# Mixture-of-experts blocks of 32 tokens in four column groups instead of 64 tokens in two

## The reference

```python
def grouped_moe(h, router_w, router_bias, w1, w3, w2):
    s = jax.nn.sigmoid((h @ router_w).astype(jnp.float32))
    ...                                   # best group of 4 experts, best 2 in it, weights wts
    combine = jnp.sum(jax.nn.one_hot(idx, N_EXPERTS) * wts[..., None], axis=1)
    for e in range(N_EXPERTS):
        he = (jax.nn.silu(h @ w1[e]) * (h @ w3[e])) @ w2[e]
        out = out + combine[:, e:e + 1] * he
```

```
layer 0: 83 69 44 52 91 105 52 24 81 70 62 63 55 57 65 51
layer 1: 11 31 42 52 25  35 40 26 12 14  7 27 73 40 60 17
```

## Time and profile before

| | |
|---|---|
| median of the runs | 1326.32 us |
| the profiled execution: its own time / span | 1325.98 us / 1324.2 us |
| PE busy / granted clock, mean | 1071.6 us (81%) / 0.882 of full speed |
| PEld, DVE, ACT, POOL busy | 490.0, 470.8, 230.0, 159.9 us |
| mean DMA rate | 240 GB/s |
| experts, layer 0: first product to barrier passed | 487.60 to 777.12 us |
| experts, layer 1: first product to barrier passed | 1062.32 to 1304.70 us |

### The profile page before, as it was taken

The page is one execution under the profiler, slowest core; times in us unless marked ns, Lnnn a source line. Parts: engine busy times, 40 slices in busy tenths (PEclk is TensorE's granted clock), DMA queues, the critical chain, the costliest instruction groups (busy, mean ns, idle before and its releaser), DMA issues. The chain is left out here.

```text
span 1324.2 us, 13657 instructions
## 1 busy us (share of the span) xinstructions
PE 1071.6 (81%) x4448; PEld 490.0 (37%) x4449; DVE 470.8 (36%) x902; ACT 230.0 (17%) x451; POOL 159.9 (12%) x272
## 2 busy tenths in 40 slices
PE   3899999777677649999998918998768489788891
PEld 1344444355444423333333306453553433223230
DVE  1167405666231432222222245624733412112223
ACT  2101121354210101111111102112520111111110
POOL 2111000000100001221221121000010012111111
PEclk8999999786688759999999968998869599888896
DMA  9978777800200534898989659113004479999973
GB/s 345 370 244 283 279 274 275 334 1 1 80 16 16 223 126 163 342 422 365 425 359 423 254 197 380 65 64 143 1 4 164 166 272 420 400 417 422 418 321 121
DMA packets 69134, 317.64 MB, mean 240 GB/s; under 512 B 7596, under 2 KB 7832, under 8 KB 55516
## 3 DMA queue, kind: packets, MB, share of 16 engines
q1 hardware_dynamic: 55760, 284.70, 54.6%
q0 software_dynamic: 9568, 20.54, 4.4%
q10 hardware_dynamic: 3756, 11.73, 2.3%
HBM read 311.10 MB, written 14.75 MB: 246 GB/s over the span
## 5 line engine op out<-in xcount | busy, mean ns | idle before, releaser
L1481 PE MATMUL ps<-ring,area 128*64 128x512 f32 x1296 | 301.0, 615 | 20.7 <-DMA ring<-in_w 16.8
L1481 PE MATMUL ps<-ring,HT 128*128 128x512 f32 (+1 forms) x672 | 295.1, 596 | 4.8 <-issue 3.0
L1481 PE MATMUL ps<-area 128*64 128x512 f32 (+5 forms) x904 | 251.6, 532 | 18.1 <-DVE area L1408 12.3
L1481 PEld LDWEIGHTS ps<-ring,HT 128*128 128x128 f32 x672 | 128.7, 195 | 158.0 <-issue 154.8
L1481 PEld LDWEIGHTS ps<-ring,area 128*64 128x64 f32 x1296 | 91.9, 141 | 189.6 <-issue 171.5
L1426 DVE COPY area<-ps 128x512 f32<-128x512 f32 x42 | 29.0, 691 | 330.1 <-PE ps L1698 330.1
L1481 PEld LDWEIGHTS ps<-area 128*64 128x64 f32 (+2 forms) x904 | 114.3, 200 | 53.3 <-issue 30.0
L1481 PE MATMUL ps<-HT,area 128*64 128x512 f32 x208 | 97.4, 623 | 10.0 <-DMA area<-in_w 10.0
L956 ACT ACTIVATE area<-ps 64x512 f32<-64x512 f32 x40 | 23.7, 592 | 432.1 <-PE ps L1481 432.1
L1060 DVE SCALAR_TENSOR_TENSOR area<-area,CW 128x512 f32<-128x512 f32 (+1 forms) x120 | 68.8, 614 | 3.9
L956 ACT ACT_TABLE_LOAD x40 | 51.3, 1283 | 41.9 <-DVEq L1419 41.2
(11 more groups left out here) (180 smaller groups left out, 814.3 us busy)
## 6 DMA issues: line engine op xcount, KB each, us to landing
ring<-in_w SPq DMA_DIRECT2D x66, 2048.0 KB, 10.2
ring<-in_w_ada SPq DMA_DIRECT2D x24, 2048.0 KB, 14.4
ring<-in_w_in SPq DMA_DIRECT2D x10, 2048.0 KB, 20.1
HT<-in_w SPq DMA_DIRECT2D x10, 2048.0 KB, 10.4
area<-in_w SPq DMA_DIRECT2D x10, 2048.0 KB, 10.5
area<-in_w SPq DMA_DIRECT2D x20, 1024.0 KB, 8.4
ring<-in_w_out SPq DMA_DIRECT2D x4, 2048.0 KB, 14.8
area<-expert_rows ACTq DMA_DIRECT2D x12, 512.0 KB, 6.7
```

The lines of the kernel that those rows point to most:

```text
L1481: return t_.matmul(out, lhsT, rhs, start=first, stop=last_)
```

## The change

`SLOT` becomes 32, so NG = 4 column groups and NW = 256: groups 0 and 1 take the two halves of w1, groups 2 and 3 those of w3; in the second product each group takes 256 of the 1024 outputs. A gather moves 128 quarter rows. NCH, the number of 128-column pieces in NW, falls from 4 to 2 and with it the transposes per block. `CB` becomes 52 (`BMAX` 48 and 4), `PEEL` 4. w2 is laid out so that a partition reads two pieces of 8 KB instead of one of 16 KB.

The gathered rows and ym get two buffers each, used in turn, with one semaphore per buffer. DVE now copies the gathered rows from xg to `xs` (`copy_x`), and PE transposes xs. gather(n) waits for the copy of block n-2. POOL works in pairs of blocks, and the number of pairs is (blocks + 3) >> 1, so that POOL gathers and scatters a few blocks past the last one; their rows are all out of bounds.

```diff
-SLOT = 64
+SLOT = 32
-CB = BMAX + 1
-PEEL = 3
+CB = BMAX + 4
+PEEL = 4
...
-        w2_v = A["w2"].rearrange("l e (p k) n -> l e p k n", p=P)
+        w2_v = A["w2"].rearrange("l e (a p k) n -> l e p a k n", p=P, a=2)
...
-                def gather(n):
+                def gather(n, r):
 
-                    if not isinstance(n, int) or n:
-                        hold(pool, xt_full[l], n, pool_passed)
-                    g.tensor_copy(gidx, TG[:, bass.ds(n, 1)]).then_inc(gidx_set[l], 1)
+                    if not isinstance(n, int) or n >= 2:
+                        hold(pool, xs_rdy[l], n - 1, pool_passed)
+                    g.tensor_copy(gidx[r], TG[:, bass.ds(n, 1)]).then_inc(gidx_set[l], 1)
...
-                blocks = pool.value_load(nb[0:1, E_N:E_N + 1], min_val=E_N, max_val=BMAX)
+                pairs = pool.value_load(nb[0:1, E_N + 1:E_N + 2], min_val=PEEL, max_val=BMAX // 2 + 2)
...
-                with pool.Fori(PEEL, blocks + 1) as n:
-                    gather(n)
-                    scatter(pool.snap(sent))
-                    pool.reg_add(sent, sent, 1)
-                for t in range(2):
-                    scatter(pool.snap(sent) + t)
-                hold(pool, scat[l], 16 * blocks, pool_passed)
+                with pool.Fori(PEEL // 2, pairs) as i:
+                    for r in range(2):
+                        gather(2 * i + r, r)
+                        scatter(pool.snap(sent) + r, r)
+                    pool.reg_add(sent, sent, 2)
+                for t in range(PEEL):
+                    hold(pool, scat[l][t % 2], pool.snap(sent) * 8 + 16 * (t // 2), pool_passed)
+                    scatter(pool.snap(sent) + t, t % 2)
+                for r in range(2):
+                    hold(pool, scat[l][r], 16 * pairs, pool_passed)
...
+                dve.drain()
+                v.tensor_scalar(nbi[:, 0:1], nb[:, E_N:E_N + 1], 3.0, None, ALU.add)
+                dve.drain()
+                v.tensor_scalar(nb[:, E_N + 1:E_N + 2], nbi[:, 0:1], 1, None, ALU.arith_shift_right)
...
+                def copy_x(n):
+
+                    if isinstance(n, int):
+                        dve.wait_ge(gath[l][n % 2], 16 * (n // 2) + 16)
+                        at_ = n % 2 * NW
+                    else:
+                        hold(dve, gath[l][0], 16 * ((n + 2) // 2), dve_passed)
+                        hold(dve, gath[l][1], 16 * ((n + 1) // 2), dve_passed)
+                        at_ = n % 2 * NW
+                    v.tensor_copy(xs, xg[:, bass.ds(at_, NW)]).then_inc(xs_rdy[l], 1)
...
-                    v.tensor_copy(ym, ps[:, B_W2, :]).then_inc(y_rdy[l], 1)
+                    if isinstance(m, int):
+                        if m >= 2:
+                            dve.wait_ge(scat[l][m % 2], 16 * (m // 2))
+                    else:
+                        hold(dve, scat[l][0], 16 * (m // 2), dve_passed)
+                        hold(dve, scat[l][1], 16 * ((m - 1) // 2), dve_passed)
+                    v.tensor_copy(ym[:, bass.ds(m % 2 * NW, NW)], ps[:, B_W2, 0:NW]).then_inc(y_rdy[l], 1)
...
                     v.tensor_copy(gT.rearrange("p c s -> p (c s)"), ps[:, B_GT, 0:NCH * 64]).then_inc(gt_rdy[l], 1)
-
+                    copy_x(b + 2)
+
+                copy_x(0)
                 copy_xT(0)
+                copy_x(1)
...
                 copy_y(dve.snap(copied))
+                dve.drain().then_inc(y_rdy[l], 3)
...
-                    hold(pe, gath[l], 16 * n + 16, pe_passed)
+                    hold(pe, xs_rdy[l], n + 1, pe_passed)
                     for a in range(NCH):
-                        last = t_.transpose(ps[:, B_XT, a * P:(a + 1) * P], xg[:, a * P:(a + 1) * P], ident)
+                        last = t_.transpose(ps[:, B_XT, a * P:(a + 1) * P], xs[:, a * P:(a + 1) * P], ident)
```

More of the change, by code:

```diff
@@ L349, in hybrid_moe_kernel @@
         nbi = cut(E_N).bitcast(i32)
-        nb = cut(E_N + 1).bitcast(i32)
+        nb = cut(E_N + 2).bitcast(i32)
         TG = cut(CB).bitcast(i32)
@@ L353, in hybrid_moe_kernel @@
         TW = cut(CB)
-        gidx = cut(1).bitcast(i32)
-        sidx = cut(1).bitcast(i32)
-        xg = cut(NW)
+        gidx = [cut(1).bitcast(i32) for _ in range(2)]
+        sidx = [cut(1).bitcast(i32) for _ in range(2)]
+        xg = cut(2 * NW)
+        xs = cut(NW)
         YM_AT = at[0]
@@ L362, in hybrid_moe_kernel @@
         gT = cut(NCH * 64).rearrange("p (c s) -> p c s", c=NCH)
-        ym = cut(NW)
+        ym = cut(2 * NW)
         EX_AT = max(at[0], 2816)
@@ L437, in hybrid_moe_kernel @@
         nb_ready = sem("counts_ready")
-        gath = sems("tokens_gathered", DEPTH)
+        gath = [sems(f"tokens_gathered_{l}", 2) for l in range(DEPTH)]
+        xs_rdy = sems("tokens_copied", DEPTH)
         xt_full = sems("xT_product", DEPTH)
@@ L447, in hybrid_moe_kernel @@
         y_rdy = sems("y_copied", DEPTH)
-        scat = sems("y_scattered", DEPTH)
+        scat = [sems(f"y_scattered_{l}", 2) for l in range(DEPTH)]
         dve_passed = sem("dve_waits_passed")
@@ L724, in gather @@
                     hold(pool, gidx_set[l], n + 1, pool_passed)
-                    pool.indirect_dma_start(xg, None, h2_rows, bass.IndirectOffsetOnAxis(ap=gidx, axis=0),
-                                            bounds_check=routed(l) * NG - 1, oob_is_err=False).then_inc(gath[l], 16)
-                def scatter(m):
+                    pool.indirect_dma_start(xg[:, r * NW:(r + 1) * NW], None, h2_rows, bass.IndirectOffsetOnAxis(ap=gidx[r], axis=0),
+                                            bounds_check=routed(l) * NG - 1, oob_is_err=False).then_inc(gath[l][r], 16)
@@ L730, in scatter @@
+                def scatter(m, r):
                     hold(pool, y_rdy[l], m + 2, pool_passed)
-                    g.tensor_copy(sidx, TS[:, bass.ds(m, 1)]).then_inc(sidx_set[l], 1)
+                    g.tensor_copy(sidx[r], TS[:, bass.ds(m, 1)]).then_inc(sidx_set[l], 1)
                     hold(pool, sidx_set[l], m + 1, pool_passed)
-                    pool.indirect_dma_start(y_rows, bass.IndirectOffsetOnAxis(ap=sidx, axis=0), ym, None,
-                                            bounds_check=2 * routed(l) * NG - 1, oob_is_err=False).then_inc(scat[l], 16)
+                    pool.indirect_dma_start(y_rows, bass.IndirectOffsetOnAxis(ap=sidx[r], axis=0), ym[:, r * NW:(r + 1) * NW], None,
+                                            bounds_check=2 * routed(l) * NG - 1, oob_is_err=False).then_inc(scat[l][r], 16)
@@ L736, in _ @@
                 for n in range(PEEL):
-                    gather(n)
-                blocks = pool.value_load(nb[0:1, E_N:E_N + 1], min_val=E_N, max_val=BMAX)
+                    gather(n, n % 2)
+                pairs = pool.value_load(nb[0:1, E_N + 1:E_N + 2], min_val=PEEL, max_val=BMAX // 2 + 2)
                 sent = pool.alloc_register(f"pool_blocks_{l}")
                 pool.reg_mov(sent, 0)
-                with pool.Fori(PEEL, blocks + 1) as n:
-                    gather(n)
-                    scatter(pool.snap(sent))
-                    pool.reg_add(sent, sent, 1)
```

8 lines of the change are left out of this document (3 added, 5 removed).

## The result

The changed kernel takes 1315.49 us (median; 1310.0 to 1317.96) beside 1325.16 for the kernel before in the same runs: ratio 0.9917, 95% interval 0.9897 to 0.9937. It is faster by 9.7 us; 26 were forecast. The profiled execution lies at 1315.83, its span is 1314.0 against 1324.2.

A forecast was written before the change was run, and what follows sets the result against it. TensorE was taken to bound layer 0 and the weights layer 1; from 1325.98, -27.5 (layer 0), -12.5 (layer 1), +3.3 (starts) and +10.5 (stage ends) sum to -26, so 1300 us, range 1284 to 1332.

The forecast's parts named there:

- The block, 6.1: Both expert stages: a 32-token block takes 24 steps of 0.215 plus 0.94, 6.1 us; first product 3.6, second 1.9.
- Rival (b): Expert products: weight loads don't hide, step 0.272, block 7.5, total 1351 us; chance 0.13 together with other slower ways.
- rival (a): Expert products: TensorE's sequencer binds, priced at a step of 0.25 and block of 6.9, total 1323 us; chance 0.09.
- Rival (c): Expert stages: POOL or the gather and scatter transfers bind, block 6.9, total 1323 us; chance 0.08.
- half the transposes fall away ... leaving 0.94: Each block: the 1.28 us lost between steps to transposes and the changes around them shrinks to 0.94.
- The weights have become the bound, the last product ends near 740: Layer 0: weight loads bind instead of TensorE; last product near 740 instead of 767.7, -27.5 us.
- behind it stand two blocks and the last second product: Layer 0's end: 14.8 us of work remain after w3 of expert 15 lands at 725.5.
- Rival (d): Weight loads in both layers: 2% slower from 8 KB w2 pieces and more indirect DMAs, +8, 1308 us; chance 0.10.
- The forecast's 5.4: Layer 0 weight stream: 5.4 us per load over 36 issues, from w2 of expert 3 to w2 of expert 15.
- Layer 1, -12.5: Layer 1's expert stage: weights bind before and after; earlier stream start and shorter work behind the last w3 give -12.5 us.
- Empty scatters, +10.5: Ends of both stages: trailing empty scatters delay the last issue by 6.3 and 4.2 us, +10.5.
- Starts, +3.3: Stage starts: copy xs, tiny DVE operations and larger tables cost 1.9 in layer 0 and 1.4 in layer 1.

The follow-up runs named there:

- e1: Changed kernel with two tiny transposes in place of the two TensorE drains at an expert's first block; 1311.81 us, ratio 0.9913.
- e8: Changed kernel, drains kept, each expert weight load cut to a small part, only layer 0 read; 254.63 us from first product to last y copy.
- e9: Changed kernel with expert weight loads cut to a small part and without the drains, only layer 0 read; 246.46 us from first product to last y copy.
- e10: Changed kernel with full weight loads but only two of eight row groups of the first product made; layer 0 247.93 us from first product to last y copy.
- e11: Kernel before with blocks of 32 tokens and the new w2 layout, without second buffers or copy xs; 1379.18 us.
- e12: Changed kernel with blocks of 64 tokens again, keeping second buffers, copy xs and the loop of block pairs; 1342.88 us, ratio 1.014.
- e4: Kernel before, blocks of 64 tokens, with the changed kernel's drains put in at experts' first blocks; 1333.85 us, ratio 1.0079.

## Why the prediction was wrong

- **The block, 6.1: right.** 6.09 inside an expert, products 3.66 and 1.93, a step 0.215. Rival (b) (weight loads don't hide, 0.272 a step) and rival (a) (0.25) are out. The step's eight instructions went out one each 0.027, twice as densely as any row before had shown. Of the two ways that the Trainium skill names (TensorE: Matmul & The Clock Gate, What happens when you issue a matmul), the 62 ns of a matmul decoded in microcode would have made a step 0.248. The trace, with 0.215, agrees with the hardware decoder alone.
- **Rival (c): out.** Mid-stage waits of TensorE for gathered rows are absent, a gather lands in 6.5 (median) and 8.2 at most in e1; y copies waited 4.3 in layer 0 for scatters, off the path.
- **The block between experts: wrong, and hidden.** The step "half the transposes fall away ... leaving 0.94" overlooked the drains that take their place at each expert's first block, 0.69 a pair by e8 and e9. As long as the weights bind they cost nothing clear of noise in layer 0 (e1).
- **"The weights have become the bound, the last product ends near 740": right mechanism, two terms mis-sized. This is the step that failed.** From e1, which has the blocks as forecast: the rate, 5.49 instead of 5.4 per load, +3.4; and "behind it stand two blocks and the last second product", 14.8 behind the landing of expert 15's w3, +6.3. The load on which the end really hangs is expert 14's w3, with five blocks behind it. The forecast's own numbers would have shown 2.4 of the 6.3: 720.7 less four loads is 699.1, plus 10.2 to landing is 709.3, and five blocks are 14.8 + 3 x 6.1 = 33.1, so 742.4. From that landing e1 needed 36.4, not 33.1: 1.6 is the clock, which the forecast let fall in layer 1's end and not here, and 1.5 the last block, which takes 16.3 from expert 15's first product to the last y copy, where TensorE waits 1.1 for the copied hidden rows instead of 0.5 and the copy starts 0.86 behind the product. (The last 0.8 are the rate and the landing of these loads and the tiny transposes.) The loads were weighed against the blocks behind them for the last expert alone.
- **Rival (d), slower loads: not by the w2 layout.** In layer 1, where the weights bind in both kernels, the 32 loads from w1 of expert 5 to w2 of expert 15 take 5.28 each before and 5.27 after. The forecast's 5.4 came from the last nine loads of layer 0, and the mean of 5.58, which it also had, served as a bound alone. In e1 the first 16 of the 36 loads take 5.60 each and the last 20 take 5.41; in e10, where TensorE doesn't hold them up, 5.60 and 5.38. In e1 the DMA engines are busy in both parts (0.99 from 530 to 567, 1.01 from 650 to 690) but move 396 and 421 GB/s. What slows the first part stays open.
- **Layer 1, -12.5: right** (-13.3), and by its terms: the stream is 5.0 earlier behind the first product (forecast 5.5), the loads give 0.5, and what stands behind the last issue is 7.8 shorter (forecast 1.3 + 6.4).
- **Empty scatters, +10.5: right, but the end cost 3.3 more** (+13.8). From the last y copy to the last scatter's DMA it is 6.0 and 4.2 more, as forecast. The rest lies behind the last scatter, which the forecast left as before: 9.60 and 6.77 to the read back, 7.12 and 5.65 before. It goes with the blocks of 32 tokens: e11, without empty scatters and second buffers, has 9.42 and 6.80, e12, with blocks of 64, 6.93 and 5.81. Why is open.
- **Starts, +3.3: not shown.** The first was nothing in sum. The +2.3 before layer 1 is over 285 us of mostly untouched code, which took between 283.7 and 290.8 in the executions of this case.
- The untouched front of the kernel was 3.8 slower in this execution; without it the profiled difference is -14. The first product of layer 0 came between 486.2 and 492.8 in the executions of all kernels here, so the 3.8 is no effect of the change that is shown.

In sum, by stretches: -17.2 - 13.3 + 13.8 + 2.3 + 3.8 + 0.4 = -10.2, the difference of the spans. Of the 16 by which it misses the forecast, 10.3 are layer 0, 3.3 the ends and 3.8 the front; the other stretches take back 1.4.

## What to carry to other kernels

When a change moves the bound from an engine to a stream, don't work out the new end from the last load alone: walk every load against all the work that stands behind it, since a cluster of long items near the end binds earlier than the last item. Read at the same time how long the stream waits for the engine (48.6 us before, 28.8 after, 23.6 in e1): that bounds what a faster engine can do for the last issue. It is an upper bound only, since a wait can pass while another load is still in flight: 25.0 less of it brought the last issue 11.2 nearer to the first product (236.7 in e1 instead of 247.9), and the other 6.6 came from the shorter work behind it. And if a loop is cut in half, look for what else rode on its iterations: here two releases fell off the transposes and became drains, hidden where the weights bind and 8.2 us in layer 0 where TensorE bounds (e8 less e9; 4.4 in e4).

## What the runs showed of the hardware

- Two drains of TensorE in a row, between products, cost 0.52 to 0.64 (e4) and 0.69 (e8 less e9, plus the 0.15 of the two transposes in their place); an increment on a 32x32 transpose costs some 0.08.
- Behind waits of 3.57 and 1.97 for weights e1's next products took 5.06 and 5.28, with the clock granted at 0.71 and 0.67, instead of 3.66 at 1.00; in layer 1, where TensorE waits often, it stood at 0.80 from 1120 to 1240.
- TensorE took four-group steps of 32-wide loads and 256 columns at 0.215 for whole stages, with clock 1.00 and 219.59 of 220 us busy.
- An indirect scatter whose entries are all out of bounds costs GpSimd the same 2.1 as a real one.
- A stream of 2 MB loads, two in flight, with the DMA engines busy throughout, took 5.27 a load in layer 1 and 5.38 to 5.60 in layer 0; in e1's layer 1 each landed 9.6 to 10.9 after its issue.
